# Sequence 0 turned un-normalised, its 1/rms multiplied in at the read-outs of the in-projection

## Chip, core and metric

The kernel runs on one core of a Trainium2 chip. The metric is the device time of one execution in microseconds (us), lower is better. Before the change the median of three runs is 1139.7 us.

## What is computed

One layer of a bidirectional encoder, applied with the same weights to two sequences of 512 tokens and 1024 channels (x_prompt is sequence 0, x_sample sequence 1), all in f32:

```
def rms_norm(x, g):
    y = xf * lax.rsqrt(jnp.mean(xf * xf, axis=-1, keepdims=True) + EPS)
    return (y * g).astype(x.dtype)

h = rms_norm(x, norm_attn_g)
proj = h @ w_in                  # 1024 -> 2304 columns: qa ka va qb kb vb
ya = global_gqa_attention(rope(rms_norm(qa)), rope(rms_norm(ka)), va)
yb = neighbourhood_attention(qb, kb, vb, nat_rel_bias, rows)
y = jnp.concatenate([rms_norm(ya, out_norm_a_g), rms_norm(yb, out_norm_b_g)], axis=-1)
x = x + y @ w_out
u = jnp.square(jax.nn.relu(rms_norm(x, norm_mlp_g) @ w_up))
return rms_norm(x + u @ w_down, final_norm_g)
```

## The kernel before

Tokens lie on partitions in eight tiles of 128, four for each sequence (NT = 8, TPB = 4). A product of two f32 matrices is made of three matmuls of rounded parts (hi times hi, lo times hi, hi times lo, in a one-pass type), the lines L1066, L1067 and L1068. So both factors have to be split into a hi and a lo part. ScalarE makes the hi parts, VectorE the lo parts.

**The input norm and the first products.** For a tile t of sequence 0 the steps are: SP issues the DMAs of its two halves of 512 columns into `pj` (L682); ScalarE squares the tile with a running sum (L905) and takes the root of the mean (L909); VectorE makes the reciprocal (L936) and multiplies the tile by it into `xn` (L945); TensorE turns `xn` in eight blocks of 128x128 against the identity `ident`, four to a PSUM bank (L966, function `pe_norm`); ScalarE casts each bank to the hi part of `hT` (L928), VectorE subtracts for the lo part (L951). Gains are multiplied into the weights: a weight piece is 128 rows (channels) of `w_in` by 512 columns; ScalarE makes `w_hi` (L1007), VectorE `w_lo` (L1016). `norm_alone` writes out this order for tiles 0 to 3 on ScalarE and VectorE, with the split of weight piece t behind tile t. Here and below, turn t means the eight transposes of tile t.

TensorE's first wave is written out by hand: turn 0; then for i = 0 to 3: turn i + 1 (up to 3), and the products that tile i and weight piece i make possible, namely 1, 3, 5 and 7 products of three matmuls (product groups 0 to 3, with 3, 9, 15 and 21 matmuls). The three products of group 1 are, in order: tile 1 with piece 0, tile 1 with piece 1, tile 0 with piece 1. Group 2 begins with tile 2 and pieces 0, 1, 2. Then turn 4, and `run_block` goes through the remaining pieces.

**Blocks.** `BLOCKS` lists the stages of the in-projection. Block 0: qa of sequence 0, banks 0 to 3. Block 1: qa of sequence 1, banks 4 to 7. Block 2: ka and va of both (256 columns). Block 3: qb, block 4: kb, with channels on partitions and tokens along the row, four banks for sequence 0 (0 to 3) and four for sequence 1 (4 to 7), in the order 0, 4, 1, 5, ... Blocks 5 and 6: vb. Each block has eight weight pieces (k = 0 to 7). Sequence 1's tiles are normed and turned between the pieces of block 0 (`woven`). At a block's last piece ScalarE and VectorE read the banks out (`take`): in qb and kb ScalarE takes sequence 0 and VectorE sequence 1, elsewhere even and odd banks. `after_tm` and `after_fm` are TensorE's waits for those read-outs when the next block reuses a bank. POOL's `stage` rounds qb and kb of a head pair later.

**DMA.** All transfers are issued by SP, in one queue. The four raw slots of weight pieces (`w_raw`) are freed by the VectorE split; `load_piece` waits for that from the fifth piece on, and everything behind it in SP's program waits too. The order at the start: both halves of tile 0, w_gain, ident, then tile 1, piece 0, tile 2, piece 1, tile 3, pieces 2 and 3, tiles 4 to 7, pieces 4 to 7.

## Time and profile before

| | us |
|---|---|
| median of 3 runs | 1139.7 (1139.53 to 1140.13) |
| profiled execution, its own time | 1139.17 |
| its span, first to last instruction | 1137.4 |
| TensorE busy | 1119.9 (98%) |
| VectorE busy | 767.7 (67%) |
| ScalarE busy | 535.6 (47%) |
| POOL busy | 186.1 (16%) |

The profile is of one execution. Times in its views count from the first instruction. Busy time of TensorE is modelled at the ends of matmuls: in a stream each is shown longer than the distance to the next, so distances between starts are the better measure. A plain f32 matmul is recorded as two, a transpose and a matmul of rounded parts as one. DMA issues are rows of SPq, and their duration is that of the issue; the time to landing is in a view of its own.

### The profile page before, as it was taken

Reading aid. Unit: us, or ns where it says so; the run is one execution under the profiler, and the core shown is the slowest. Engines: PE = TensorE matmul, PEld = TensorE weight load, DVE = VectorE, ACT = ScalarE, POOL = GpSimd, SP = SyncE. Lnnn points to the kernel's source line nnn. Section 1 sums busy time; section 2 is a strip of 40 time slices with the busy share of each in tenths; the row PEclk is TensorE's granted clock in tenths of the full one; section 3 lists DMA queues with packets and bytes.
Section 4 is the critical chain, followed back from the end, with each engine's and each line's share of the span. In section 5 each row is a group of like instructions: output and inputs, shape, how many; then the busy total and the mean of one; then the engine's idle time right before and its main releaser. Section 6 shows DMA issues by size and latency. Waiting matters only on the chain.

```text
span 1137.4 us, 15392 instructions
## 1 busy us (share of the span) xinstructions
PE 1119.9 (98%) x5536; PEld 929.7 (82%) x5536; DVE 767.7 (67%) x1348; ACT 535.6 (47%) x1018; POOL 186.1 (16%) x199
## 2 busy tenths in 40 slices
PE   6999999999999999999999999999999999999997
PEld 5898888789999988888888788888888888888885
DVE  5525314477666556464977998948859769579497
ACT  6421213366676645255334446245254353452556
POOL 2430496121214000200100100001001001000012
PEclk9999999999999999999999999999999999999999
DMA  9422113475445352421210210221111112102204
GB/s 262 119 74 56 47 47 84 112 166 112 85 95 118 111 143 88 162 84 56 75 37 1 75 49 26 75 75 38 51 62 57 54 39 75 56 19 75 75 19 148
DMA packets 55387, 90.97 MB, mean 80 GB/s; under 512 B 6032, under 2 KB 23440, under 8 KB 55312
## 3 DMA queue, kind: packets, MB, share of 16 engines
q1 hardware_dynamic: 55312, 89.99, 28.5%
q8 instruction: 44, 0.72, 0.3%
q14 instruction: 31, 0.25, 0.1%
HBM read 68.97 MB, written 4.19 MB: 64 GB/s over the span
## 4 chain that ended last, share of the span: by engine, by line
PE 97%; DVE 1%; ACT 1%; issue 0%; DMA 0%; DVEq 0%; SPq 0%; ACTq 0%
PE ps L1066 27%; PE ps L1068 27%; PE ps L1067 27%; PE ps L1274 5%; PE ps L1296 2%; PE ps L966 1%; PE ps L1232 1%; PE ps L1247 1%; PE ps L1233 1%; PE ps L1216 1%; PE ps L1259 1%; DMA pj<-x_prompt 0%; PE ps L1193 0%; PE ps L1451 0%; PE ps L1311 0%
## 5 line engine op out<-in xcount | busy, mean ns | idle before, releaser
L1066 PE MATMUL ps<-w_hi,uv_hi 128*128 128x512 f32 x448 | 178.6, 399 | 0.2 <-issue 0.2
L1066 PE MATMUL ps<-hT,w_hi 128*128 128x512 f32 x448 | 177.1, 395 | 0.0
L1068 PE MATMUL ps<-w_hi,uv_lo 128*128 128x512 f32 x448 | 176.8, 395 | 0.0
L1068 PE MATMUL ps<-hT,w_lo 128*128 128x512 f32 x448 | 176.8, 395 | 0.0
L1067 PE MATMUL ps<-hT,w_hi 128*128 128x512 f32 x448 | 176.8, 395 | 0.0
L1067 PE MATMUL ps<-w_lo,uv_hi 128*128 128x512 f32 x448 | 176.7, 394 | 0.0
L1016 DVE SCALAR_TENSOR_TENSOR w_lo<-w_raw,w_gain,w_hi 128x512 fp32r<-128x512 f32 (+1 forms) x88 | 69.8, 798 | 140.6 <-ACT w_hi L1007 139.8
L2051 DVE TENSOR_TENSOR xr<-ps,xr 128x512 f32<-128x512 f32 x220 | 138.0, 683 | 7.4 <-PE ps L1068 7.0
L1007 ACT ACTIVATE w_hi<-w_raw,w_gain 128x512 fp32r<-128x512 f32 (+1 forms) x88 | 61.4, 704 | 171.5 <-PE ps L1068 168.0
L1066 PE MATMUL ps<-w_hi,hT 128*128 128x512 f32 (+1 forms) x320 | 120.4, 376 | 0.3 <-DVE hT L951 0.2
L1068 PE MATMUL ps<-w_hi,hT 128*128 128x512 f32 (+1 forms) x320 | 119.1, 372 | 0.0
L1067 PE MATMUL ps<-w_lo,hT 128*128 128x512 f32 (+1 forms) x320 | 119.0, 372 | 0.0
L2533 POOL TENSOR_TENSOR sqf<-sqf 128x512 f32<-128x512 f32 x16 | 20.4, 1297 | 502.9 <-DVE w_lo L1896 502.9
L1066 PEld LDWEIGHTS ps<-w_hi,uv_hi 128*128 128x128 f32 x448 | 84.3, 188 | 22.1 <-issue 2.3
L1067 PEld LDWEIGHTS ps<-w_lo,uv_hi 128*128 128x128 f32 x448 | 84.4, 188 | 20.4 <-issue 1.0
L1068 PEld LDWEIGHTS ps<-w_hi,uv_lo 128*128 128x128 f32 x448 | 84.3, 188 | 19.8
L1068 PEld LDWEIGHTS ps<-hT,w_lo 128*128 128x128 f32 x448 | 84.3, 188 | 19.8
L1067 PEld LDWEIGHTS ps<-hT,w_hi 128*128 128x128 f32 x448 | 84.3, 188 | 19.8
L1066 PEld LDWEIGHTS ps<-hT,w_hi 128*128 128x128 f32 x448 | 84.3, 188 | 19.6
L1917 DVE TENSOR_TENSOR uv_lo<-sqf,uv_hi 128x512 fp32r<-128x512 f32 x112 | 75.1, 713 | 14.7 <-ACT uv_hi L1589 13.9
L1589 ACT CAST uv_hi<-sqf 128x512 fp32r<-128x512 f32 x112 | 64.6, 616 | 22.1 <-DVE sqf L2039 20.1
L1497 ACT CAST w_hi<-turn 128x512 fp32r<-128x512 f32 x64 | 36.6, 617 | 75.3 <-PE ps L1068 75.3
(164 smaller groups left out, 2005.9 us busy)
## 6 DMA issues: line engine op xcount, KB each, us to landing
w_raw<-w_in SPq DMA_DIRECT2D x48, 256.0 KB, 2.7
stk<-stg SPq DMA_DIRECT2D x32, 256.0 KB, 3.6
w_raw<-w_out SPq DMA_DIRECT2D x32, 256.0 KB, 2.6
raw<-w_down SPq DMA_DIRECT2D x32, 256.0 KB, 2.9
turn<-w_down SPq DMA_DIRECT2D x32, 256.0 KB, 2.8
w_raw<-w_up SPq DMA_DIRECT2D x24, 256.0 KB, 2.7
turn<-w_up SPq DMA_DIRECT2D x24, 256.0 KB, 2.9
raw<-w_up SPq DMA_DIRECT2D x24, 256.0 KB, 3.0
```

What stands on the lines that cost most here:

```text
L1007: ins = nc.scalar.mul(w_hi[:, slot, 0:width], src, g)
L1016: ins = nc.vector.scalar_tensor_tensor(w_lo[:, slot, 0:width], src, g, hi, ALU.mult, ALU.subtract)
L1066: nc.tensor.matmul(out, a_hi, b_hi, start=first, stop=False, skip_group_check=onto)
L1067: nc.tensor.matmul(out, a_hi, b_lo, start=False, stop=False, skip_group_check=onto)
L1068: return nc.tensor.matmul(out, a_lo, b_hi, start=False, stop=last, skip_group_check=onto)
L1274: mm = nc.tensor.matmul(ps[a_out_bank(u // TPB)][:, q * VW:(q + 1) * VW], turn_slot(u - q + k)[:, q * P:(q + 1) * P], pj[:, b * TPB + k, c ...
L1296: mm = nc.tensor.matmul(ps[OB_BANK][:, q * VW:(q + 1) * VW], turnB[:, n % PTB_SLOTS, k * P:(k + 1) * P], v, start=(k == 0), stop=(k == nk ...
L1497: nc.scalar.copy(w_hi[:, n % W_SLOTS, :], weight(c, False, v, kt)).then_inc(hi_split, 1)
L1589: nc.scalar.copy(uv_hi[:, u_slot(c, name), kt, :], u_source(name, kt)).then_inc(uv_hi_ready, 1)
L1917: nc.vector.tensor_tensor(uv_lo[:, u_slot(c, name), kt, :], u_source(name, kt), uv_hi[:, u_slot(c, name), kt, :].bitcast(F32), ALU.subtrac ...
L2051: nc.vector.tensor_tensor(dst, ps[v % 2 * 4 + t][:, :], dst, ALU.add).then_inc(c_added, 1)
L2533: nc.gpsimd.tensor_tensor(sqf[:, 1, kt, :], sqf[:, 1, kt, :], sqf[:, 0, kt, :], ALU.subtract).then_inc(s4_done, 1)
```

## The change

Sequence 0's tiles are turned as they land, straight from `pj`, and split into hi and lo without having been divided by their RMS. The reciprocals are multiplied in when the banks of the in-projection are read out.

- In `pe_norm`, turn t of sequence 0 waits for the left half of the tile (`x_left`) ahead of its first four transposes and for the right half (`x_right`) ahead of the last four. It waits for no VectorE result. Sequence 1 is normed as before.
- ScalarE's squares of tiles 0 to 3 (`act_square_raw`) come one tile behind the casts and the weight split, and one root (`act_root_raw`) serves four tiles. VectorE makes the four reciprocals in one instruction and, in one more, a diagonal matrix of them for each tile (`diag`).
- `turn_rstd`: at block 1, k = 3, TensorE multiplies a matrix of ones (set by POOL) by the four diagonals, which puts 1/rms of token j in column j of each row of bank 0. VectorE copies it to `rstd_row` one piece later. These four products are plain f32 ones.
- Read-outs with tokens on partitions (qa, ka, va, vb of sequence 0) multiply by the tile's reciprocals in place of a copy. For qb and kb VectorE now reads out sequence 0, times `rstd_row`, and ScalarE sequence 1; the waits of TensorE and of POOL's `stage` follow. TensorE's first product of block 2 in bank 0 waits for the copy of the row.
- SP's order: left half of tile 0, ident, right half, w_gain, piece 0, and from then on a tile and a piece in turn. For tiles 4 to 7 the piece comes first.

```diff
@@ SP
-            load_x_halves(0)
+            load_x_half(0, 0)
+            sp.dma_start(ident[:, :], ident_c).then_inc(const_landed, 16)
+            load_x_half(0, 1)
             sp.dma_start(w_gain[:, :, :].rearrange("p m d -> p (m d)"), w_gains).then_inc(gain_landed, 16)
-            sp.dma_start(ident[:, :], ident_c).then_inc(const_landed, 16)
-            for t in range(1, TPB):
-                load_x_halves(t)
-                load_pieces(t - 1, t)
-            load_pieces(TPB - 1, RAW_SLOTS)
-            for t in range(TPB, NT):
-                load_x_halves(t)
-            load_pieces(RAW_SLOTS, NT)
+            load_pieces(0, 1)
+            for t in range(1, NT):
+                if t >= TPB:
+                    load_pieces(t, t + 1)
+                load_x_half(t, 0)
+                load_x_half(t, 1)
+                if t < TPB:
+                    load_pieces(t, t + 1)
@@ pe_norm
-            pe.wait_ge(xn_ready, norm_no(m, t) + 1)
+            raw = m == 0 and t < TPB
+            if not raw:
+                pe.wait_ge(xn_ready, norm_no(m, t) - TPB + 1)
...
             for j in range(2):
+                if raw:
+                    pe.wait_ge((x_left, x_right)[j][t], 16)
                 for d in range(4):
+                    cols = slice((4 * j + d) * P, (4 * j + d + 1) * P)
                     last = nc.tensor.transpose(norm_bank(m, t, j)[:, d * P:(d + 1) * P],
-                                               xn[:, t % 2, (4 * j + d) * P:(4 * j + d + 1) * P], ident[:, :])
+                                               pj[:, t, cols] if raw else xn[:, t % 2, cols], ident[:, :])
@@ TensorE
+            def turn_rstd(k):
+                if k == ROW_TURN:
+                    pe.wait_ge(all_ones, 1)
+                    pe.wait_ge(diag_ready, 1)
+                    pe.wait_ge(act_evac, 1)
+                    for t in range(TPB):
+                        last = nc.tensor.matmul(ps[0][:, t * P:(t + 1) * P], ones[:, :], diag[:, t, :], start=True,
+                                                stop=True)
+                    last.then_inc(row_turned, 1)
+            def after_row(pos, bank):
+                if bank == 0:
+                    pe.wait_ge(row_copied, 1)
+                after_tm(0)(pos, bank)
             run_block(0, after_norm0)
-            run_block(1, after_norm0)
-            run_block(2, after_tm(0))
+            run_block(1, after_norm0, turn_rstd)
+            run_block(2, after_row)
@@ ScalarE
+        def act_square_raw(act, t):
+            norm_src_wait(act, 0, t)
+            nc.scalar.activation(qkb_0[:, 2 * t:2 * t + 2, :].rearrange("p h c -> p (h c)"), pj[:, t, 0:D], ACT.Square,
+                                 accum_out=stat[:, 0, t, 0:1]).then_inc(sumsq, 1)
...
-            norm_alone(0, 0, square, hT_hi_of, lambda n: act_split(act, n, n % W_SLOTS, width_of(n), piece_gain(n)))
+            for t in range(TPB):
+                hT_hi_of(0, t)
+                act_split(act, t, t % W_SLOTS, width_of(t), piece_gain(t))
+                if t:
+                    act_square_raw(act, t - 1)
+            act_square_raw(act, TPB - 1)
+            act_root_raw(act)
@@ VectorE, take
                     if blk.what in ("qb", "kb"):
-                        ins = nc.vector.tensor_scalar(qkb[1][:, part, :], ps[bank][:, :],
-                                                      QSCALE if blk.what == "qb" else 1.0, None, ALU.mult)
+                        dve.wait_ge(row_copied, 1)
+                        ins = nc.vector.scalar_tensor_tensor(qkb[0][:, part, :], ps[bank][:, :],
+                                                             QSCALE if blk.what == "qb" else 1.0, rstd_row[:, :],
+                                                             ALU.mult, ALU.mult)
+                    elif bank < TPB:
+                        dve.wait_ge(rstd_ready, TPB)
+                        ins = nc.vector.tensor_scalar(evac_dst(blk, bank), src, rstd[:, 0, bank, 0:1], None, ALU.mult)
@@ VectorE
+                        if i == 1 and k == ROW_TURN + 1:
+                            dve.wait_ge(row_turned, 1)
+                            nc.vector.tensor_copy(rstd_row[:, :], ps[0][:, :]).then_inc(row_copied, 1)
...
-            norm_alone(0, 0, norm, hT_lo_of, lambda n: dve_split(dve, n, n % W_SLOTS, width_of(n), piece_gain(n)))
+            for t in range(TPB):
+                hT_lo_of(0, t)
+                dve_split(dve, t, t % W_SLOTS, width_of(t), piece_gain(t))
+            dve.wait_ge(rms_ready, TPB)
+            nc.vector.reciprocal(rstd[:, 0, 0:TPB, 0], rms[:, 0, 0:TPB, 0]).then_inc(rstd_ready, TPB)
+            dve.wait_ge(rstd_ready, TPB)
+            dve.wait_ge(const_landed, 16)
+            nc.vector.tensor_tensor(diag[:, :, :], over(ident[:, :], 1, TPB), over(rstd[:, 0, 0:TPB, 0], 2, P),
+                                    ALU.mult).then_inc(diag_ready, 1)
```

What SP issues first. Before, both halves of tile 0, the gains, ident; here x_prompt is sequence 0, x_sample sequence 1, and w_in a weight piece:

```order
L682 DMA pj<-x_prompt 128x1x512 x2
L701 DMA w_gain<-w_gains 128x16
L702 DMA ident<-ident_c 128x128
L682 DMA pj<-x_prompt 128x1x512 x2
L693 DMA w_raw<-w_in 128x512
L682 DMA pj<-x_prompt 128x1x512 x2
L693 DMA w_raw<-w_in 128x512
```

and with the change:

```order
L690 DMA pj<-x_prompt 128x1x512
L709 DMA ident<-ident_c 128x128
L690 DMA pj<-x_prompt 128x1x512
L711 DMA w_gain<-w_gains 128x16
L701 DMA w_raw<-w_in 128x512
L690 DMA pj<-x_prompt 128x1x512 x2
L701 DMA w_raw<-w_in 128x512
L690 DMA pj<-x_prompt 128x1x512 x2
```

ident has moved between the halves of tile 0, and piece 0 ahead of tile 1.

ScalarE at its start, before: the squares (L905) stand ahead of the casts (L928) that make `hT`:

```order
L905 ACTIVATE xn,stat<-pj 128x1024
L909 ACTIVATE rms<-stat,eps 128x1
L905 ACTIVATE xn,stat<-pj 128x1024
L909 ACTIVATE rms<-stat,eps 128x1
L928 CAST hT<-ps 128x4x128 x2
L1007 ACTIVATE w_hi<-w_raw,w_gain 128x512
```

and with the change, where L926 is the square and L932 the root of all four tiles:

```order
L951 CAST hT<-ps 128x4x128 x2
L1025 ACTIVATE w_hi<-w_raw,w_gain 128x512
L951 CAST hT<-ps 128x4x128 x2
L1025 ACTIVATE w_hi<-w_raw,w_gain 128x512
L926 ACTIVATE qkb,stat<-pj 128x1024
L951 CAST hT<-ps 128x4x128 x2
L1025 ACTIVATE w_hi<-w_raw,w_gain 128x512
L926 ACTIVATE qkb,stat<-pj 128x1024
L951 CAST hT<-ps 128x4x128 x2
L1025 ACTIVATE w_hi<-w_raw,w_gain 128x512
L926 ACTIVATE qkb,stat<-pj 128x1024 x2
L932 ACTIVATE rms<-stat,eps 128x4
```

Each square now stands behind the cast and the weight split of the tile after it.

TensorE in block 1, with the change, between pieces 3 and 4; the lines of the three matmuls are now L1084 to L1086:

```order
L1084 MATMUL ps<-w_hi,hT 128x512
L1085 MATMUL ps<-w_lo,hT 128x512
L1086 MATMUL ps<-w_hi,hT 128x512
L1190 MATMUL ps<-diag,ones 128x128 x4
L1084 MATMUL ps<-w_hi,hT 128x512
```

The four row products are new there; before, the matmuls of piece 4 followed those of piece 3.

## Rows read from the trace of the kernel before

**Rows 1.** The page: TensorE's busy time, and its busy tenths in 40 slices.
```profile
PE 1119.9 (98%) x5536; PEld 929.7 (82%) x5536; DVE 767.7 (67%) x1348; ACT 535.6 (47%) x1018; POOL 186.1 (16%) x199
...
PE   6999999999999999999999999999999999999997
```

**Rows 2.** Waits of TensorE: who for whom, us in total, times, longest.
```profile
PE ps L966 <- DVE xn L945: 9.0, 3, 8.3
PE ps L1247 <- DVE negmax L2315: 1.1, 2, 0.8
```

**Rows 3.** Chain that ended last, 0 to 20 us: start, us, what.
```profile
1.47 4.16 DMA pj<-x_prompt
...
5.65 1.16 ACT xn L905 x2
...
7.36 0.76 DVE xn L945
```

**Rows 4.** Timeline of TensorE: start, us, operation, idle before and releaser.
```profile
8.26 1.94 PE L966 MATMUL ps<-ident,xn 128*128 128x128 f32 x8 [8.26 <-DVE xn L945]
10.59 1.85 PE L966 MATMUL ps<-ident,xn 128*128 128x128 f32 x8 [0.39 <-DVE xn L945]
...
13.85 1.10 PE L966 MATMUL ps<-ident,xn 128*128 128x128 f32 x8 [0.36 <-DVE xn L945]
15.13 0.47 PE L1066 MATMUL ps<-w_hi,hT 128*128 128x512 f32 x1 [0.19 <-DVE hT L951]
...
17.31 1.03 PE L966 MATMUL ps<-ident,xn 128*128 128x128 f32 x8
18.10 0.48 PE L1066 MATMUL ps<-w_hi,hT 128*128 128x512 f32 x1
```

**Rows 5.** Stretch: PE, PEld, DVE, ACT, POOL busy; PEclk, DMA share, GB/s.
```profile
8.26:12.54 4.28, 3.79 (x16) 3.14 (x17) 2.77 (x5) 4.01 (x9) 0.00 (x0) 1.00 1.07 262
```

**Rows 6.** Timeline of SP: start and us of DMA issues.
```profile
0.73 1.31 SPq L682 DMA_DIRECT2D pj<-x_prompt  x2
...
6.27 0.59 SPq L693 DMA_DIRECT2D w_raw<-w_in  x1
...
8.12 1.06 SPq L693 DMA_DIRECT2D w_raw<-w_in  x2
```

**Rows 7.** Issue to landing, us (last number), of issues at 0.73, 2.71, 6.27, 8.12.
```profile
pj<-x_prompt SPq DMA_DIRECT2D x1, 256.0 KB, 3.6
ident<-ident_c SPq DMA_DIRECT2D x1, 64.0 KB, 3.4
w_raw<-w_in SPq DMA_DIRECT2D x1, 256.0 KB, 5.4
w_raw<-w_in SPq DMA_DIRECT2D x1, 256.0 KB, 6.2
```

**Rows 8.** Timeline of ScalarE and VectorE, 8 to 15 us.
```profile
10.24 0.59 ACT L928 CAST hT<-ps 128x512 fp32r<-128x512 f32 x1 [0.21 <-PE ps L966]
...
10.72 0.73 ACT L1007 ACTIVATE w_hi<-w_raw,w_gain 128x512 fp32r<-128x512 f32 x1
...
11.65 0.74 DVE L1016 SCALAR_TENSOR_TENSOR w_lo<-w_raw,w_gain,w_hi 128x512 fp32r<-128x512 f32 x1
...
12.71 1.05 ACT L928 CAST hT<-ps 128x512 fp32r<-128x512 f32 x2
```

**Rows 9.** Timeline of TensorE in the tail; L1451 is a plain f32 product.
```profile
1123.63 0.40 PE L1068 MATMUL ps<-w_hi,uv_lo 128*128 128x512 f32 x1
1123.86 1.02 PE L1451 MATMUL ps<-xr,ident 128*128 128x512 f32 x2
...
1124.95 0.39 PE L1067 MATMUL ps<-w_lo,uv_hi 128*128 128x512 f32 x1
```

**Rows 10.** Groups of VectorE by line: count, busy us, mean ns, idle before.
```profile
L1016 DVE SCALAR_TENSOR_TENSOR w_lo<-w_raw,w_gain,w_hi 128x512 fp32r<-128x512 f32 (+1 forms) x88 | 69.8, 798 | 140.6 <-ACT w_hi L1007 139.8
...
L1880 DVE TENSOR_SCALAR qkb<-ps 128x512 f32<-128x512 f32 x8 | 5.5, 682 | 3.3 <-PE ps L1068 3.2
```

58 lines of the change are left out of this document (34 added, 24 removed).

## Prediction

> **What bounds the kernel now.** I read the page first. TensorE is busy for 98% of the span, in all but the first and the last of the forty slices [rows 1]. So a microsecond is to be had in two ways only: TensorE gets less work, or it starts its unbroken run earlier. The list of waits says where it does not run: of its idle time 9.0 us lie before the turns of the normalised tiles, 8.3 of them in one piece, at the start [rows 2]. The chain of waits over the first 20 us names what fills that piece: tile 0 lands at 5.63 (1.47 + 4.16), ScalarE squares it (1.16), the root and the reciprocal follow, VectorE scales it (0.76), and the turn starts at 8.26 [rows 3, 4]. The timeline of TensorE then shows four more turns and the first products [rows 4]: 10.59 turn 1, 13.85 turn 2, 15.13 the nine matmuls of group 1 (2.18 us until turn 3), 17.31 turn 3, 18.10 group 2 (fifteen matmuls). From 15.13 on TensorE has no gap that the list of waits would show, so **the start of group 2, 18.10, is my yardstick**: whatever moves it moves everything behind it, since the only later wait of TensorE over 1 us in that list, 1.1 on VectorE in the attention part [rows 2], is for an engine that itself follows TensorE. From 8.26 to 12.54 the DMA engines are full (share 1.07, 262 GB/s) [rows 5], which will matter.
>
> A second reading of the same rows: eight turns take 1.94 and 1.85 us at first, 1.10 at 13.85 [rows 4], though the granted clock is printed as full [rows 5]. That is the ratio of TensorE's two levels, 1.2 and 2.4 GHz. It was low for the 3.9 us from its first work until about 12.2, and high after.
>
> **What goes away.** Four squares, roots, reciprocals and scalings no longer stand ahead of the turns of sequence 0. The squares and one root come back behind ScalarE's casts, where nobody on the path waits: their results are wanted at the first read-out, far behind. The four scalings of VectorE (0.76 each) vanish. What is late next is the data itself.
>
> **When the data lands.** Tile 0's left half was issued at 0.73 and landed 3.6 later, at 4.3; ident needed 3.4 from issue to landing [rows 6, 7]. It is now second in SP's queue. As it is 64 KB behind 256 it lands about 4.6 (bounds: 4.3, were it free, and 1.47 + 3.4 = 4.9), so turn 0 starts at 4.7. The right half follows ident and lands near 5.9. For the tiles behind I count bytes, since the engines are full and the queue is worked off in order. Weight piece 1 landed at 6.27 + 5.4 = 11.7, piece 2 at 8.12 + 6.2 = 14.3 [rows 6, 7]. What stood ahead of and in piece 1 (three tiles, ident, gains, two pieces) is what now stands ahead of and in the right half of tile 2, so that half lands at 11.7. In the same way the right half of tile 3 lands at 14.3, and tile 1's one such step (2.6 us) before tile 2's, at 9.1. Each x tile after the first is thus later than before by one weight piece.
>
> **TensorE's new start.** Turn 0 ends near 7.0; turn 1's right half runs from 9.1 to 10.1 at the low level (half of 1.85). The weight chain behind it: cast 0.59, w_hi 0.73, w_lo 0.74 [rows 8], so piece 1 is split at 12.1 or 12.2. Product group 0 fits between 10.1 and 11.4 even at the low level. Turn 2's right half, from 11.8, takes half of 1.10: 12.3. So group 1 starts at 12.3 rather than 15.13, bound by a landing and with the weight split just ahead of it. Then 2.18 for it and 0.79 for turn 3 (17.31 to 18.10) [rows 4]: 15.3. Tile 3 has landed by 14.3. Piece 2's chain on ScalarE (square 1.2, two casts 1.05, w_hi 0.73, then w_lo 0.74 [rows 3, 8]) ends at 15.1, and only the third product of group 2 wants it. **18.10 - 15.3 = 2.8 us** earlier. If transfers come 0.3 sooner, the weight split binds and it is 3.0. I take off 0.1 for executions in which the level is still low at 11.8 (turn 2's second half would cost 0.5 more).
>
> **What SP now does in another order.** It waits for a free raw slot ahead of each of pieces 4 to 7, with x tiles of sequence 1 queued behind each such wait. The waits end when pieces 0 to 3 are split (about 9, 12, 15, 18), while the DMA engines still have work queued until about 18, so they don't run dry; the bytes until piece 7 are the same. Turn 4 wants its tile landed, squared, scaled by 23.7; the tile lands at about 18 and its chain takes 2.5. Nothing is charged. Without that cover it would be up to 1 us.
>
> **What is added on the path.** Four products of 128 x 128 stand in TensorE's stream in block 1, in plain f32. The nearest row is the plain f32 product of the tail: from the matmul at 1123.63 to the one at 1124.95 there are 1.32 us, in which stand that matmul (0.23), one plain product of 512 columns, recorded as two halves of 0.43, and one more matmul (0.23) [rows 9]. So 0.86 us for 512 columns, and the four products have 512 columns together: **0.87 us**. The bounds are 0.44 (as cheap as the turns, 0.11 for 128 columns) and 1.3 (each of the eight halves bound by its 0.19 us weight load with no overlap). I take 0.87, the same type and kind.
>
> The Trainium skill (TensorE: Matmul & The Clock Gate, Terms) says that the transpose mode is 4 times faster for FP32 than an ordinary product. Here the turn takes 0.11 us for 128 columns and the plain product 0.22, so this trace shows 2 times. By the page the four products would cost 1.74, and the time would be 0.9 later than I forecast.
>
> **What is added beside the path.** The diagonal (one 128x512 operation of VectorE, some 0.8) and its reciprocal lie after piece 3's split, and TensorE wants them 25 us later. The copy of the row (0.69) lies in block 1 and is wanted a few us later, at bank 0 of block 2. The read-outs of block 0, 2 and vb do the same pass with a scale. For qb and kb the two engines swap sequences and VectorE multiplies by the row: an operation with two inputs took it 798 ns on average, a read-out with a constant 682 [rows 10]. Four of them, one in 1.4 us, are hidden by the products of the next bank. Zero, all of it; the POOL waits follow the swap. If VectorE were the bound there it would be eight times 0.12, 1 us.
>
> **Sum.** -2.8 + 0.1 + 0.9 = -1.8 us. On the profiled execution (span 1137.4, its own time 1139.17) that gives 1137.4. The median of the runs shown, 1139.7, is 0.5 above that execution, and the result will be a median too: **1139.7 - 1.8 = 1137.9 us**. A measurement of this kernel can tell about 0.2% (2.3 us) from no change, so the forecast itself lies within it.
>
> **Rivals.**
> - *More gain than I count.* Landings 0.3 sooner, the row products at 0.6: -3.0 + 0.6 = -2.4, 1137.3. For it: ident and the gains are small. Against: the byte count is of this very queue. Chance 0.17.
> - *The level rises late.* In the change TensorE pauses from 7.0 to about 7.8, and again for landings before turn 2, where it paused for 0.4 before. If the rise comes at the end of group 1, turn 2's half costs 0.5 more and the nine matmuls twice 2.18 less what is saved, about 2.0 more: 2.5 in all, hence -2.8 + 2.5 + 0.9 = +0.6, 1140.3; if it comes halfway, 1138.9. I take 1139.0 for this case. Chance 0.12.
> - *Plain f32 product at four times the turn.* 1138.8. Only the page speaks for it. Chance 0.05.
> - *Slower.* The same mechanism, further: the pauses keep the level low through turn 3 and group 2. Group 2 (15 matmuls of 0.235) would take 3.5 more and turn 3 0.8 more, on top of the 2.5: -2.8 + 6.8 + 0.9 = +4.9, 1144.6. It decides from the place where the rise falls: later than the middle of group 2 the kernel is slower by over 0.2%. Against it: the level rose before across a pause of 0.4 and another soon after didn't drop it. Chance 0.04.
> - *It doesn't start earlier.* Something I take as covered holds the first wave (the weight split of piece 1, SP's waits), and the gain only pays for the row products: 1139.7. Chance 0.07.
>
> The Trainium skill (TensorE: Matmul & The Clock Gate, What's actually happening) says that the low level is the default, that activity releases it, and that the watch runs free of the kernel's start. By it the moment of the rise differs from run to run, and the second and fourth cases may show in single executions; the trace of one execution can't show that.
>
> **The numbers.** Forecast 1137.9 has 0.55. Faster by over 0.2% (below 1137.4): the first rival and a small part of the forecast's own spread, 0.21. Slower by over 0.2%: 0.05. The rest, 0.74, is within. The range 1137.1 to 1139.1 holds the forecast, the first rival, the f32 case and half of the late rise.
>
> **What the profile after would show.** The first turn at 4.7 and in halves; turn 2's right half starting on a landing near 11.7; group 1 at 12.3, group 2 at 15.3; from there a constant lead of 2.8 until block 1, then 1.9 after four products that take 0.87; no wait of TensorE at bank 0 of block 2. If group 2 starts at 15.3 and the total is not 1.8 shorter, something later took it back, which I hold impossible. The prediction is wrong if the turns of tile 2 still take 0.2 each, or if group 1 starts on a weight split later than 12.3.

## The result, and the profile of the changed kernel

| | median us (lowest to highest) | executions |
|---|---|---|
| before | 1139.79 (1139.53 to 1140.13) | 6 |
| changed | 1144.37 (1141.12 to 1145.15) | 6 |

The ratio is 1.0034, with a 95% interval of 1.0021 to 1.0047. The changed kernel is slower by 0.34%, some 4 us (4.6 between the medians); 1137.9 was forecast. A second measurement gave it 1141.27 (1139.25 to 1145.71, 12 executions) against 1139.62, ratio 1.0018 (1.0008 to 1.0028). It is slower in both, and its executions spread over 4 to 6.5 us where those of before spread over 0.6 to 2. That spread is part of the finding.

The profiled execution is the lowest of the first six: its own time is 1141.12, its span 1139.1, against 1137.4 before. The page, TensorE's busy time and its tenths in 40 slices, to be read beside [rows 1]:

```profile
PE 1122.6 (99%) x5544; PEld 930.6 (82%) x5544; DVE 765.3 (67%) x1343; ACT 535.3 (47%) x1015; POOL 185.9 (16%) x200
...
PE   7999999999999999999999999999999999999997
```

TensorE has eight matmuls more, as four plain f32 products are recorded in halves, and its first slice went from 6 to 7 tenths: it does begin earlier. Its waits (who for whom, us in total, times, longest), to be read beside [rows 2]:

```profile
PE ps L994 <- DMA ident<-ident_c: 4.5, 1, 4.5
PE ps L994 <- DMA pj<-x_prompt: 2.2, 4, 1.5
PE ps L994 <- DVE xn L968: 1.3, 1, 1.3
```

Of the 9.0 us before turns, 6.7 are left at the start, and now they are waits for DMAs. The third row is new. L968 scales the tiles of sequence 1, whose norm the change leaves as it was, and before there was no wait for such a tile. The timeline of TensorE, to be read beside [rows 4]:

```profile
4.49 1.12 PE L994 MATMUL ps<-ident,pj 128*128 128x128 f32 x4 [4.49 <-DMA ident<-ident_c]
...
8.41 1.12 PE L994 MATMUL ps<-ident,pj 128*128 128x128 f32 x4 [1.48 <-DMA pj<-x_prompt]
...
12.82 0.66 PE L994 MATMUL ps<-ident,pj 128*128 128x128 f32 x4 [0.28 <-DMA pj<-x_prompt]
13.24 0.48 PE L1084 MATMUL ps<-w_hi,hT 128*128 128x512 f32 x1
...
16.20 0.48 PE L1084 MATMUL ps<-w_hi,hT 128*128 128x512 f32 x1
...
37.15 1.09 PE L994 MATMUL ps<-ident,xn 128*128 128x128 f32 x8 [1.34 <-DVE xn L968]
...
52.21 1.05 PE L1190 MATMUL ps<-diag,ones 128*128 128x128 f32 x8
53.02 0.48 PE L1084 MATMUL ps<-w_hi,hT 128*128 128x512 f32 x1
```

Turn 0 starts at 4.49 and group 2 at 16.20, 1.9 us before the 18.10 of before. Late in block 0 stands the surprise: turn 7 comes after 1.34 us in which TensorE has nothing to do. I laid the matmuls of the two traces side by side, each against its counterpart. The changed kernel leads by 1.90 us from group 2 on and by 0.34 behind turn 7. The first product of block 1 costs it 0.17 more, and the row products 0.82, so that it is 0.65 late behind them. By 210 us it is 1.1 late, and 1.4 at the last product, with no wait that is new. Of the 0.43 between the row and 210 us some 0.3 turned out to be systematic (the row, below).

The chain of waits names what holds turn 7 (start, us, what):

```profile
22.56 0.67 DVE w_lo L1034
23.25 9.78 DMA w_raw<-w_in
33.10 0.58 issue
33.68 1.06 ACT hT L951 x2
34.74 1.06 ACT xn L916 x2
35.82 0.30 ACT rms L920
36.34 0.77 DVE xn L968
37.15 1.09 PE ps L994 x8
```

To be read backwards: turn 7 waits for tile 7 scaled by VectorE, that for ScalarE's root and square, these for the two casts of turn 5, and the casts for a weight piece. A tile of x has nothing to do with a weight piece. The timeline of ScalarE shows why (start, us, operation, idle before and releaser):

```profile
28.85 0.29 ACT L920 ACTIVATE rms<-stat,eps 128x1 f32<-128x1 f32 x1
33.05 0.72 ACT L1025 ACTIVATE w_hi<-w_raw,w_gain 128x512 fp32r<-128x512 f32 x1 [3.91 <-DMA w_raw<-w_in]
33.68 1.06 ACT L951 CAST hT<-ps 128x512 fp32r<-128x512 f32 x2
34.63 1.07 ACT L916 ACTIVATE xn<-pj 128x1024 f32<-128x1024 f32 x1
```

ScalarE works in order. It stands 3.91 us before the split of **weight piece 8**, whose own products begin only with block 1, at 40.96, and behind it are queued the casts of turn 5 and the square of tile 7. The square is what TensorE will want next. The same place in the kernel before, ScalarE's timeline and the issue of piece 8 (at 25.80, last number: us to landing):

```profile
30.23 0.30 ACT L909 ACTIVATE rms<-stat,eps 128x1 f32<-128x1 f32 x1
30.66 0.72 ACT L1007 ACTIVATE w_hi<-w_raw,w_gain 128x512 fp32r<-128x512 f32 x1
```

```profile
w_raw<-w_in SPq DMA_DIRECT2D x1, 256.0 KB, 4.8
```

Before, ScalarE was free at 30.53 and the piece landed at 30.64, a tenth later: ScalarE had no slack, and a wait too short to show in the view. With the change ScalarE is there at 29.14 and the piece lands at 33.0. It is issued 2.55 us earlier (23.25) and lands 2.4 later, as the queue takes 9.8 us to get to its end rather than 4.8.

TensorE did have slack there before. VectorE's scaling of tile 7 and TensorE's turn 7:

```profile
33.95 0.75 DVE L945 TENSOR_SCALAR xn<-pj,rstd 128x1024 f32<-128x1024 f32 x1
```

```profile
37.55 1.04 PE L966 MATMUL ps<-ident,xn 128*128 128x128 f32 x8
```

Tile 7 was ready at 34.70, 2.85 us ahead of its turn. A lead of 1.90 uses up two thirds of that and leaves 0.95. Tile 7 is now ready at 37.11, 2.41 later, so TensorE has to come out some 1.5 later against its counterpart. That is what the side-by-side reading shows (1.90 less 0.39 at the first transpose of turn 7); the idle time in the view, 1.34, is shorter because ends of matmuls are modelled. So it takes both, the earlier start and the later landing. With the lead of 2.8 that was forecast, nothing would have been left even at the old landing.

### The profile page after: what moved, and what is told of

It is laid out like the page before. It is cut to its first block, busy times and chain, and to the rows that moved or that the text cites. A ratio compares the mean times of both kernels' runs of the same rounds, so it can differ in the third digit from the quotient of the medians.

```text
span 1139.1 us, 15426 instructions
## 1 busy us (share of the span) xinstructions
PE 1122.6 (99%) x5544; PEld 930.6 (82%) x5544; DVE 765.3 (67%) x1343; ACT 535.3 (47%) x1015; POOL 185.9 (16%) x200
## 3 DMA queue, kind: packets, MB, share of 16 engines
q1 hardware_dynamic: 55312, 89.99, 28.5%
## 4 chain that ended last, share of the span: by engine, by line
PE 95%; DMA 1%; ACT 1%; DVE 1%; issue 0%; SPq 0%; DVEq 0%; ACTq 0%
PE ps L1084 27%; PE ps L1085 27%; PE ps L1086 27%; PE ps L1309 5%; PE ps L1331 2%; PE ps L1267 1%; PE ps L1282 1%; PE ps L1268 1%; PE ps L1251 1%; PE ps L1294 1%; PE ps L994 1%; DMA w_raw<-w_in 1%; DMA pj<-x_prompt 1%; PE ps L1228 0%; PE ps L1486 0%
## 5 line engine op out<-in xcount | busy, mean ns | idle before, releaser
L1084 PE MATMUL ps<-w_hi,uv_hi 128*128 128x512 f32 x448 | 178.5, 399 | 0.2 <-issue 0.2
L1084 PE MATMUL ps<-hT,w_hi 128*128 128x512 f32 x448 | 177.1, 395 | 0.0
L1086 PE MATMUL ps<-hT,w_lo 128*128 128x512 f32 x448 | 176.8, 395 | 0.0
L1086 PE MATMUL ps<-w_hi,uv_lo 128*128 128x512 f32 x448 | 176.8, 395 | 0.0
L1084 PE MATMUL ps<-w_hi,hT 128*128 128x512 f32 (+1 forms) x320 | 121.0, 378 | 0.0
L1086 PE MATMUL ps<-w_hi,hT 128*128 128x512 f32 (+1 forms) x320 | 119.2, 372 | 0.0
L1084 PEld LDWEIGHTS ps<-w_hi,uv_hi 128*128 128x128 f32 x448 | 84.3, 188 | 22.1 <-issue 2.0
L1086 PEld LDWEIGHTS ps<-w_hi,uv_lo 128*128 128x128 f32 x448 | 84.3, 188 | 19.9
L1086 PEld LDWEIGHTS ps<-hT,w_lo 128*128 128x128 f32 x448 | 84.3, 188 | 19.9
L1084 PEld LDWEIGHTS ps<-hT,w_hi 128*128 128x128 f32 x448 | 84.3, 188 | 19.8
```

Of the source, the lines that this page charges most:

```text
L1084: nc.tensor.matmul(out, a_hi, b_hi, start=first, stop=False, skip_group_check=onto)
L1086: return nc.tensor.matmul(out, a_lo, b_hi, start=False, stop=last, skip_group_check=onto)
```

## The experiments

Three theories stood at the start. **A, data late**: the transfers of pieces and tiles late in block 0 come later and are wanted earlier; whatever brings piece 8 sooner, or takes its split out of ScalarE's way, removes the wait before turn 7. **B, the row**: the row products and what hangs on them in blocks 1 and 2 cost more than their 0.82 us. **C, the level**: TensorE's low level lasts longer in executions with many short waits at the start.

The table is for looking up; the sections say what follows. Piece 3, tile 7 and piece 8 are landings, "wait" is TensorE's before turn 7, all in us in the profiled execution. The median and the ratio to before (95% interval) are those of all executions. Chips differ between the groups of runs, so medians of different groups are best compared by their ratios.

| kernel | piece 3 | tile 7 | piece 8 | group 2 | wait | median | ratio |
|---|---|---|---|---|---|---|---|
| before | 15.2 | 23.7 | 30.6 | 18.10 | 0 | 1139.79 | |
| before_again | 15.5 | 24.0 | 31.1 | 18.07 | 0 | 1140.06 | 1.0005 (0.9995 to 1.0015) |
| changed | 16.3 | 28.3 | 33.0 | 16.20 | 1.3 | 1144.37 | 1.0034 (1.0021 to 1.0047) |
| same_again | 17.0 | 32.0 | 36.2 | 16.76 | 3.9 | 1141.27 | 1.0018 (1.0008 to 1.0028) |
| tables_late | 16.2 | 26.8 | 27.9 | 17.21 | 0 | 1139.59 | 1.0000 (0.9992 to 1.0009) |
| old_order | 15.4 | 24.0 | 31.1 | 16.62 | 0 | 1140.74 | 1.0009 (1.0001 to 1.0018) |
| no_row | 15.7 | 27.8 | 33.0 | 15.76 | 1.7 | 1139.36 | 0.9996 (0.9988 to 1.0005) |
| defer_split | 16.4 | 29.8 | 33.7 | 16.07 | 0 | 1140.40 | 1.0006 (0.9997 to 1.0016) |
| late_turned_row | 16.9 | 28.7 | 29.9 | 16.64 | 0 | 1139.11 | 0.9993 (0.9983 to 1.0002) |
| late_busy | 16.6 | 29.6 | 30.0 | 16.13 | 0 | 1139.32 | 0.9996 (0.9987 to 1.0005) |
| late_old_order | 17.7 | 26.4 | 31.0 | 18.15 | 0 | 1140.60 | 1.0006 (0.9997 to 1.0016) |
| late_all | 16.2 | 27.7 | 28.1 | 16.14 | 0 | 1139.38 | 1.0000 (0.9991 to 1.0009) |
| row_twice | 15.9 | 27.2 | 29.0 | 15.85 | 0 | 1139.42 | 0.9997 (0.9987 to 1.0006) |
| before_late | 15.7 | 23.8 | 28.5 | 17.98 | 0 | 1139.51 | 0.9998 (0.9989 to 1.0007) |

### The changed kernel once more

No edit.

> The changed kernel once more, for a second trace and for the spread of its executions. Theory A (data late): in the first trace group 2 started 1.9 us earlier, but piece 8 of the weights landed at 33.0, ScalarE waited 3.9 us for it with the work for turn 7 queued behind, and TensorE lost 1.35 us before turn 7; the executions differ because the DMA rate of the first 35 us differs. Then the landing of tile 7's last half (28.3) and of piece 8 (33.0) should move by a microsecond or more in this trace, the wait before turn 7 with them, and the total with the wait; the executions spread over 3 us or more around 1144. Theory C (TensorE's level): the landings are the same and the extra time is in turns or matmuls at half speed.

Its profiled execution is its highest, 1145.71, and so shows what a high one is made of. TensorE's timeline around turn 7, and three stretches (PE, PEld, DVE, ACT, POOL busy; PEclk; DMA share; GB/s):

```profile
40.28 1.97 PE L994 MATMUL ps<-ident,xn 128*128 128x128 f32 x8 [3.94 <-DVE xn L968]
41.89 0.78 PE L1084 MATMUL ps<-w_hi,hT 128*128 128x512 f32 x1
42.47 0.63 PE L1085 MATMUL ps<-w_lo,hT 128*128 128x512 f32 x1
42.89 0.63 PE L1086 MATMUL ps<-w_hi,hT 128*128 128x512 f32 x1
```

```profile
36.30:40.28 3.98, 0.04 (x2) 0.01 (x1) 2.93 (x6) 3.95 (x9) 0.00 (x0) 0.99 0.51 133
40.28:43.60 3.32, 3.32 (x12) 3.03 (x13) 3.32 (x6) 2.35 (x6) 0.00 (x0) 0.50 0.52 122
43.60:46.00 2.40, 2.40 (x11) 1.94 (x11) 1.34 (x3) 1.53 (x3) 0.00 (x0) 1.00 0.76 175
```

The wait is 3.94 instead of 1.34, as piece 8 landed at 36.2. And it brings a second loss: after the pause the granted clock is 0.50, the lower of the two levels, for 3.3 us. The turn takes 1.97 instead of 1.09 and the products behind it stand 0.58 and 0.42 apart, where 0.31 and 0.23 are usual. The sum: 1.34 ahead at group 2, 3.94 waited, 1.7 lost at the low level and 0.80 at the row products make 5.1 late at 57.5 (side by side with before: 5.1 as well), and 6.3 at the last product. So A has its mechanism; C has a part in it, but as a consequence of A's wait and not at the start. Of the 18 executions of the changed kernel four were recorded with a mean granted clock of 0.996 or 0.997 over the whole span, all of them at 1144.49 or above; no execution of the kernel before lies below 0.998. That fits such a low stretch in them too. But 1144.55 and 1144.21 have 0.998, so it is not the whole of the high times.

### The tables' transfers behind those of block 1's pieces

`tables_late`: the changed kernel, in which the transfers of rope, the q/k gains, the mask and the bias tables are issued behind weight pieces 8 to 15. Nothing else is moved.

```
+            load_pieces(NT, NT + BH)
             sp.dma_start(rope[...], rope_c).then_inc(pool_landed, 16)
             ...
             for h in range(BH):
                 sp.dma_start(bias_raw[:, h, :], src).then_inc(pool_landed, 16)
-                load_pieces(NT + h, NT + h + 1)
```

> The changed kernel, but SP issues rope, the q/k gains, the mask and the eight bias tables after weight pieces 8 to 15 and not among them (1.8 MB less ahead of pieces 8 to 15; POOL needs the tables far later). Theory A: piece 8 lands near 30.5 and TensorE's wait before turn 7 is gone, so 1139.8 at most in the best executions and a median 1.4 to 4 us below the changed kernel's, with a small spread. Theory B (the added work on the path, row products and read-outs, makes the kernel slow) and theory C: no difference from the changed kernel, 1144.

ScalarE's split of piece 8:

```profile
29.63 0.72 ACT L1025 ACTIVATE w_hi<-w_raw,w_gain 128x512 fp32r<-128x512 f32 x1 [0.61 <-PE ps L1086]
```

Piece 8 lands at 27.9 (near 30.5 was expected), ScalarE waits 0.61 for TensorE and no longer for a DMA, and TensorE's wait before turn 7 is gone. The median is 1139.59 against 1141.27 for the changed kernel on the same chip, and equal to before. That is what A says. The edit also takes 0.9 MB of tables out from ahead of piece 8, and tile 7 lands 1.5 earlier in this trace, so that by itself it doesn't tell which of the two TensorE was held by; `defer_split` does. B has the row products still in it and would have left the time where it was: as the main cause it falls.

It doesn't get below before, because the start gives less than forecast. Here the level rose only at 14.9, so group 2 came at 17.21, 0.9 ahead, and the row products took that back.

### The same in the kernel before

`before_late`: the same edit in the kernel before. `before_again`: the kernel before, no edit.

> Control: the kernel before, with SP's tables behind pieces 8 to 15. In its trace piece 8 landed at 30.6, 3 us ahead of the need, and TensorE never waited for it. So theory A expects no change: 1139.7 within 0.3. A gain here would mean that the late tables are worth something of their own, and that tables_late did not cure a wait that the change brought.

> The kernel before once more, for a second trace. The changed kernels' matmuls lagged 0.1 to 0.9 us more behind the first trace of it by the end than at 60 us, without a wait. If that is in the executions and not in the change, this trace too differs from the first by some tenths over the same stretch. Transfers: the four x tiles and four pieces that landed by 15.2 in the first trace land anywhere from 15 to 18 here, as in the changed kernels, and the span still moves by less than 1 us, because the first products stand behind the norm.

Piece 8 lands at 28.5 instead of 30.6 and the time is unchanged (0.9998, 0.9989 to 1.0007). In the kernel before these transfers cost nothing; they cost only once TensorE is 2 us earlier. `before_again` is a look at the noise: from group 2 to 640 us both keep their distance to the trace of before within 0.06 us, and from there `before_again` falls 0.35 behind and `before_late` gains 0.25, with no wait that differs. A few tenths in the later half can't be given a cause by comparing two traces; a step in the first 210 us can.

It also showed a late level in the kernel before (TensorE's timeline):

```profile
12.57 0.76 PE L1066 MATMUL ps<-w_hi,hT 128*128 128x512 f32 x1
...
13.99 1.08 PE L966 MATMUL ps<-ident,xn 128*128 128x128 f32 x8
15.10 0.47 PE L1066 MATMUL ps<-w_hi,hT 128*128 128x512 f32 x1
```

Product group 0 at the low level takes 0.57 and 0.42 between starts, and yet group 1 stands at 15.10 as in [rows 4] (15.13): before, VectorE's and ScalarE's chain set the start, and it covered the slow matmuls. The changed kernel has no such cover.

### The order of x and weights of before

`old_order`: the changed kernel, with x tiles and weight pieces issued in the order of before.

```
-            load_pieces(0, 1)
-            for t in range(1, NT):
-                if t >= TPB:
-                    load_pieces(t, t + 1)
+            for t in range(1, TPB):
                 load_x_half(t, 0)
                 load_x_half(t, 1)
-                if t < TPB:
-                    load_pieces(t, t + 1)
+                load_pieces(t - 1, t)
+            load_pieces(TPB - 1, RAW_SLOTS)
+            ...
```

> The changed kernel with the old order of x tiles and weight pieces in SP's program (tile 1, piece 0, tile 2, piece 1, tile 3, pieces 2 and 3, tiles 4 to 7, pieces 4 to 7; ident still between the halves of tile 0). Theory A: the same bytes stand ahead of piece 8, so it lands late too, and the median stays within 1 us of the changed kernel's 1144. If the interleaving itself slows the queue (the x tiles took 1.2 to 1.4 us a half and not 1.1), tile 7 and piece 8 land 1 to 2 us sooner here and the time falls to 1141 or 1142. Theories B and C: 1144.

TensorE's timeline:

```profile
10.67 0.77 PE L1085 MATMUL ps<-w_hi,hT 128*128 128x512 f32 x1 [1.20 <-DVE w_lo L1035]
...
13.65 0.49 PE L1085 MATMUL ps<-w_hi,hT 128*128 128x512 f32 x1
```

Tile 7 lands at 24.0 and piece 8 at 31.1, as in the kernel before, and the wait before turn 7 is gone. Theory A as I had put it, by the bytes ahead of piece 8, missed here; the other branch, that the interleaving itself is slower, came true. At the start TensorE now waits 1.2 for the split of piece 0 instead of for x, and group 2 stands at 16.62, 0.4 later. So the interleaved order buys 0.4 us at the start and costs the transfers behind it 2 to 4. Its median, 1140.74, is 0.5 below the changed kernel's and 1.1 above before. Side by side with before it leads by 1.5 at group 2 and loses 0.3 at the first product behind turn 4, which needs weight piece 4 (landed at 24.6, as before): the earlier start meets that transfer too. It leads by 0.35 behind the row products, and is 0.6 late at the end; the profiled execution, 1139.96, is also one of its lower ones. What the higher ones wait for wasn't traced.

### The row left out

`no_row`: the four products of ones and diagonals are left out, and VectorE copies the diagonals themselves in place of the row. So q and k of the neighbourhood attention in sequence 0 are multiplied by the diagonals, mostly zeros, in place of 1/rms; all other work is done.

```
-            run_block(1, after_norm0, turn_rstd)
+            run_block(1, after_norm0)
```

> The changed kernel without the four row products of TensorE: VectorE copies the diagonals themselves into rstd_row, so qb and kb of sequence 0 are multiplied by a wrong row and the output is not the reference's. It measures the price of the products: 0.87 us by the forecast, 0.82 by the first trace (the lag of the matmuls behind those of the kernel before grows by that in block 1). The total falls by 0.8 to 0.9, within the spread of the executions. Theory B has them cost 2 us or more, with what waits for the row.

The wait stays:

```profile
PE ps L994 <- DVE xn L968: 1.7, 1, 1.7
```

So B isn't what holds turn 7. But it has more in it than I forecast. The step of 0.82 at 52 us is gone, and with it most of the 0.43 that the changed kernel loses between there and 210 us: here it is 0.15. The place of it is in block 2, whose matmuls have 256 columns. TensorE's timeline at two matmuls of it, with 140 starts from one to the other; before, then the changed kernel:

```profile
69.22 0.28 PE L1066 MATMUL ps<-w_hi,hT 128*128 128x256 f32 x1
...
85.83 0.28 PE L1068 MATMUL ps<-w_hi,hT 128*128 128x256 f32 x1
```

```profile
70.01 0.28 PE L1084 MATMUL ps<-w_hi,hT 128*128 128x256 f32 x1
...
86.81 0.28 PE L1086 MATMUL ps<-w_hi,hT 128*128 128x256 f32 x1
```

16.61 us against 16.80, or 118.7 ns from one start to the next against 120.0. In `no_row` it is 118.7 again. All other traces of the changed kind show 120.0, and all three of the kernel before 118.7. Over the 192 matmuls of block 2 that is 0.25 us. The first product behind the row adds 0.07. So the row costs about 1.15 us, not 0.82. Why a block that begins 11 us behind the row runs 1% slower isn't known: `late_turned_row` and `row_twice` below narrow it a little. The median falls by 1.9 against the changed kernel on this chip, where 0.8 to 0.9 was expected; with executions between 1137.1 and 1141.7 I put no cause to the other 0.75.

### The split of piece 8 moved behind the norm of tile 7

`defer_split`: the transfers stay as changed. In ScalarE's and VectorE's programs the split of piece 8 is moved to the place of piece 9's.

```
-                            act_split(act, n, n % W_SLOTS, width_of(n), piece_gain(n))
+                            for late in () if n == 8 else (8, 9) if n == 9 else (n,):
+                                act_split(act, late, late % W_SLOTS, width_of(late), piece_gain(late))
```

> The changed kernel with one thing moved: ScalarE and VectorE make the hi and lo parts of weight piece 8 one step later, after the casts of turn 5, the square and the scaling of tile 7 (k = 5 of block 0), together with piece 9. SP's queue is as in the changed kernel, so piece 8 still lands as late, at 33 or later. Theory A says that this landing costs time only because the cast of turn 6 and the square of tile 7 stand behind the split of piece 8 in ScalarE's order: then TensorE's wait before turn 7 (1.3 and 3.9 us in the two traces) is gone, the median falls to 1139.7, and the spread is under 2.5 us. If TensorE is held by the late bytes themselves (tile 7 or piece 8 wanted at once), the wait stays, and so does the median of 1141 to 1144.

ScalarE, and then TensorE at the first product of block 1:

```profile
33.76 0.72 ACT L1025 ACTIVATE w_hi<-w_raw,w_gain 128x512 fp32r<-128x512 f32 x1 [1.78 <-DMA w_raw<-w_in]
```

```profile
39.67 0.47 PE L1084 MATMUL ps<-w_hi,hT 128*128 128x512 f32 x1 [0.36 <-DVE hT L974]
```

This is the run that separates the late transfer from the order in which ScalarE meets it. Piece 8 lands at 33.7, later than in the changed kernel's first trace, and still TensorE doesn't wait before turn 7, for the square and root of tile 7 (30.50 to 31.98) are done by then. A small wait comes in its place, as the queue of work behind the two splits is now late for block 1. The median is 1140.40 and the ratio 1.0006 (0.9997 to 1.0016), against 1.0018 for the changed kernel: most of the loss is back, as far as runs on two chips can be compared. The median of 1139.7 and the spread under 2.5 us that were expected did not come: the executions lie between 1139.2 and 1142.7.

### The row by transposes

`late_turned_row`: `tables_late`, and the row of 1/rms is made by transposing four matrices, each of which holds in all 128 columns of a row the 1/rms of that row's token, instead of by plain f32 products.

```
-                        last = nc.tensor.matmul(ps[0][:, t * P:(t + 1) * P], ones[:, :], diag[:, t, :], start=True,
-                                                stop=True)
+                        last = nc.tensor.transpose(ps[0][:, t * P:(t + 1) * P], diag[:, t, :], ident[:, :])
...
-            nc.vector.tensor_tensor(diag[:, :, :], over(ident[:, :], 1, TPB), over(rstd[:, 0, 0:TPB, 0], 2, P),
-                                    ALU.mult).then_inc(diag_ready, 1)
+            nc.vector.tensor_copy(diag[:, :, :], over(rstd[:, 0, 0:TPB, 0], 2, P)).then_inc(diag_ready, 1)
```

> tables_late (the tables of SP behind pieces 8 to 15), and the row of 1/rms made by turning: VectorE writes 1/rms across 128 columns in place of the diagonal, and TensorE turns these four tiles against ident in place of four plain products with ones. Forecast of the rows: a plain f32 product of 128 columns 0.22 us, a turn 0.11, so the lag that the matmuls get at this place falls from 0.82 to 0.44 and the total by 0.4 against tables_late (1139.2). If the products cost what they do for another reason (the change of operands, the weight load), the lag stays at 0.8.

```profile
50.90 0.60 PE L1190 MATMUL ps<-ident,diag 128*128 128x128 f32 x4
51.26 0.48 PE L1084 MATMUL ps<-w_hi,hT 128*128 128x512 f32 x1
```

From the transposes to the next product there are 0.36 us, where the plain products took 0.81 (52.21 to 53.02). By the measure that gave 0.82 before, the lag that the matmuls get here is 0.36, and 0.44 at the second one behind, as expected. The 0.43 behind the row stay. It is the lowest median of all, 1139.11 (1139.2 was expected), at 0.9993 (0.9983 to 1.0002) of before. That is not more than no change, but it is the form I would use.

`row_twice` is this kernel with each of the four transposes done twice, to see what block 2's pace hangs on.

```
-                    for t in range(TPB):
+                    for t in (0, 1, 2, 3, 0, 1, 2, 3):
```

> Tables' transfers behind the pieces of block 1, the row of 1/rms made by transposes, and each of the four transposes is done twice: eight instructions of TensorE in block 1, k = 3. The question is what makes the 256-column matmuls of block 2 stand 120.0 ns apart in all kernels that make the row, and 118.7 ns where it isn't made. If it follows from the number of TensorE's instructions ahead (their place in the program), eight transposes may bring 118.7 back or keep 120.0, but with one or the other the first product behind the row changes as well; if it follows from the row being made at all, block 2 stays at 120.0. The eight transposes take 0.79 us where four took 0.36, and the median is 0.4 above that of the kernel with four, 1139.5, within 0.2% of before.

```profile
50.10 1.04 PE L1190 MATMUL ps<-ident,diag 128*128 128x128 f32 x8
50.89 0.48 PE L1084 MATMUL ps<-w_hi,hT 128*128 128x512 f32 x1
```

Eight transposes take 0.79 us, the time that the four f32 products took in their eight halves, and the median is 1139.42. Block 2 keeps its 120.0 ns with four transposes, with eight, and with f32 products. So neither the form nor the number of the instructions sets the pace; what `no_row` lacks besides them are TensorE's three waits ahead of them, and these weren't taken out by themselves.

### Idle products ahead of the data

`late_busy`: `tables_late`, and TensorE multiplies ones by ones 7 times before ident lands and 4 times behind turn 0, into a bank that is overwritten.

```
+            def keep_busy(n):
+                for _ in range(n):
+                    nc.tensor.matmul(ps[0][:, 0:P], ones[:, :], ones[:, :], start=True, stop=True)
+            pe.wait_ge(all_ones, 1)
+            keep_busy(7)
             pe.wait_ge(const_landed, 16)
...
             pe_norm(pe, 0, 0)
+            keep_busy(4)
```

> tables_late with eleven idle products of TensorE (ones by ones, into bank 0 which is cleared later): seven from about 1.2 us until ident lands and four after turn 0. Theory A gives the start of group 1 to the landing of tile 2 (12.7 to 13.0) and, in tables_late, to turns and products at the low level until 12 to 14.9. With earlier work the level should be high from about 8 on: product group 0 takes 0.7 and not 1.3, turn 2's halves 0.5 each, group 1 starts within 0.6 of tile 2's landing, 13.2, and group 2 at 16.2 rather than 17.2; total 0.5 to 1 us below tables_late. If the level doesn't matter, no change.

```profile
1.14 3.36 PE L1142 MATMUL ps<-ones 128*128 128x128 f32 x14 [1.14 <-POOL ones L2482]
...
10.11 0.47 PE L1084 MATMUL ps<-w_hi,hT 128*128 128x512 f32 x1
...
12.67 0.66 PE L994 MATMUL ps<-ident,pj 128*128 128x128 f32 x4 [0.29 <-DMA pj<-x_prompt]
13.08 0.48 PE L1084 MATMUL ps<-w_hi,hT 128*128 128x512 f32 x1
```

The level is high from 6.0 on. The turns behind that and group 0 take half, and group 1 still stands at 13.08, where the changed kernel had it at 13.24: the right half of tile 2 lands in between. Against that trace C is worth 0.2 us at the start; what binds is the data. Against `tables_late`, where the level rose only at 14.9, group 2 comes 1.1 earlier (16.13, as expected, for 17.21). Of the 0.5 to 1 us expected in the median 0.3 came (1139.32 for 1139.59), and the intervals of the two overlap.

### Two combinations

`late_old_order` is `tables_late` with the order of before; `late_all` is `tables_late` with the row by transposes and the idle products.

> tables_late with the old order of x tiles and weight pieces. In four traces of the new order the transfers up to piece 3 had landed at 15.7 to 17.0, in two of the old order at 15.2 and 15.4, though the bytes are the same. If the order makes the difference, piece 3 lands at 15.2 to 15.5 here too; the first product then waits for piece 0 (9.0) and its split until about 10.6, group 1 starts at 13.6, and the total is that of tables_late within 0.5 us. If the difference was chance, piece 3 lands between 15.7 and 17.

> The three edits that helped, together, on the changed kernel: tables of SP behind pieces 8 to 15, row of 1/rms by turning, and the eleven idle products of TensorE. If they add, each from its own place (no wait on piece 8; 0.4 us of row; level high from 6 us on), the median is 1138.7: late_turned_row's 1139.1 less the 0.3 to 0.6 of the idle products. That is 0.8 to 1.1 us below the kernel before, 0.1%. If the row's gain and the early level are one and the same chance of the executions, 1139.1.

`late_old_order` missed. In the profiled execution, its highest, TensorE waited 2.1 us for splits (`w_lo`), 1.4 for that of piece 0 and 0.7 at 28.36 for that of piece 4, and group 2 came at 18.15; piece 3 landed at 17.7, though the order is that of before, which had it at 15.2. So late landings in the first 17 us can come without the new order of x and weights (ident still stands between the halves of tile 0 here). The median, 1140.60, is not within 0.5 of that of `tables_late` either. `late_all` has the lowest span, 1135.9, and a median of 1139.38, no better than before: 7 of its 11 executions are above 1139.0, three of them above 1141. 1138.7, or at worst 1139.1, was expected. Two of those three were recorded with a mean granted clock of 0.996 and 0.997, so a stretch at the low level may have come back in them; none of them was traced. None of these versions beats the kernel before by more than the measurement can tell.

## Why the prediction was wrong

**What held.** Turn 0 was forecast for 4.7 and started at 4.49, on ident, in halves. The row products were forecast at 0.87 and took 0.81 where they stand. The Trainium skill's factor of four between the transpose mode and an ordinary FP32 product (TensorE: Matmul & The Clock Gate, Terms), which would have made them 1.74, did not show: four products took 0.81, four transposes 0.36 and eight 0.79, a factor of about two. The read-outs were free: no wait of TensorE stands at block 2's first bank, and VectorE's read-out with the row as second input took no longer than the one of before with a constant, 682 [rows 10]:

```profile
L1926 DVE SCALAR_TENSOR_TENSOR qkb<-ps,rstd_row 128x512 f32<-128x512 f32 x8 | 5.3, 678 | 1.9 <-PE ps L1086 1.9
```
The diagonal took VectorE 0.69 at 20.53, with nobody waiting. Two slips in the working changed nothing: eight halves bound by weight loads of 0.19 would take 1.5 us and not 1.3, and the timeline shows three more turns behind the first, not four.

**Step "When the data lands" gave 0.9 us too much.** By counting bytes I had the right half of tile 2 at 11.7, and the chain has the end of its transfer at 12.78 (6.26 + 6.52). The count was right as a count: what was transferred by then is the same set of ten transfers as by 11.7 before. It just took 1.1 us longer. The halves of tiles 1 and 2 came 1.2 to 1.6 us after the transfer before them, where the trace of before has 1.0 to 1.1. One trace gave me one rate, and I treated it as a constant. So group 1 started at 13.24 rather than 12.3 and group 2 at 16.20 rather than 15.3: a lead of 1.9 in place of 2.8. In the other traces with the new order it is between 0.9 and 2.3.

**Step "What SP now does in another order" failed.** "Nothing is charged" rested on two statements: the DMA engines don't run dry, and the bytes until piece 7 are the same. Both are so (their share from 12 to 32 us is 1.04 before and 1.06 changed). The conclusion isn't. For one thing, an equal busy share is not an equal rate. From 12 to 28.3 us the share is 1.06 in both traces, but 300 GB/s were moved before and 271 with the change.

The twelve transfers behind piece 3 (tiles 4 to 7 and pieces 4 to 7) took 10.7 to 11.1 us from its landing to the last of theirs in all five traces with the order of before, `late_old_order` among them, and 10.6 to 14.9 in the nine with the new order. In the first trace of the changed kernel they took 11.97 where they had taken 10.92. Of the 2.4 us by which piece 8 came later, 1.1 had arisen up to piece 3, 1.05 arose here and 0.2 behind. For another, I took "the queue never runs dry" for "nobody waits", and looked at tile 4 alone. Pieces 4 to 7 now stand ahead of tile 7, which moved its landing from 23.7 to 28.3, and piece 8, behind all of them and the tables, from 30.6 to 33.0. The rows I had read stopped at piece 2. One more, ScalarE's split of piece 8 at 30.66, would have shown that ScalarE had no slack there, and two more that TensorE had 2.85 us: even a landing at the old time is late for ScalarE once the work ahead of it moves up, though not yet for TensorE. With the lead of 1.9 and the landing 2.4 later TensorE lost 1.5 at turn 7, where I had put nothing.

**Step "What is added on the path" was short by 0.3.** The products themselves held; the 0.07 behind them and the 0.25 in block 2 are in no row of before.

**The yardstick.** "Whatever moves it moves everything behind it" was the sentence that hid this, and "which I hold impossible" its echo. The engine was never waiting behind group 2 *at the old pace*. A start that comes earlier meets the transfers of block 0 at their old times or, as here, later. The lead was constant only until turn 7, not until block 1.

**The rivals.** The slower case was priced at 1144.6 and given 0.04, by the low level lasting through group 2. The median came out near it, by another mechanism: a wait late in block 0, and the drop of the level that follows a long one. At the start the level rose at 11.9 in the changed kernel's first trace and at 12.9 in the second. The number is no confirmation of the rival. That the moment of the rise differs between executions did show: in the two traces of the kernel before, whose TensorE began at 8.26 and 8.22, it was 12.2 and 14.1.

**What stays open.** Of the 4.6 us between the two medians, the trace of the lowest execution accounts for its own 1.7. For the rest I have one other trace (1145.71: wait 3.9, low level 1.7), and the inference that the others lie between, since the edits that take the wait away take most of the excess with it. But those edits were measured against a changed kernel at 1141.27, 1.7 us above before; none was measured against the 1144.37 of the first measurement. Its high executions were not traced, and why it lies 3 us above the second isn't known. Why the same bytes take 1 to 2.5 us longer in the first 17 us of most changed kernels is open as well: by `late_old_order`, one trace, the order of x and weights is not its only cause. And so is why block 2 runs slower where the row is made.

## What to carry to other kernels

When a stage is made to start earlier, go through every later wait for a transfer, not only the next one, and compare its landing with the moment at which the engine *would now* ask for it; in an in-order engine the piece it waits for may be one that nobody needs yet, with urgent work queued behind. Moving transfers past each other in a full queue decides who is late, and can change the rate, even where the engines stay equally busy and the bytes are the same. The executions of the kernel before, whose start hangs on ScalarE and VectorE, spread over 0.6 to 2.2 us; those of the versions whose start hangs on landings spread over 2 to 6.5.

## What the runs showed of the hardware

- The same transfers, issued at nearly the same times, landed over a wide range: piece 3, with the same bytes ahead of it, at 15.2 to 17.7 us in fourteen traces.
- In a full queue a transfer issued 2.55 us earlier landed 2.4 later. From issue to landing piece 8 took 4.8 us before, 9.8 changed, and 12.4 in the second trace of the changed kernel.
- Weight pieces that follow one another landed 0.6 us apart (pieces 4 to 7 of before: 24.24, 24.85, 25.48, 26.10); behind an x half they took 0.5 to 0.8 in the first traces of both kernels. x halves took 1.0 to 1.1 before, up to 2.1 in the first 17 us of changed kernels (tile 1 in `late_busy`), and once 2.6 (tile 7 in `same_again`). All of them are 256 KB.
- At the same busy share of the DMA engines, 1.06 from 12 to 28.3 us, 300 GB/s were moved before and 271 changed.
- TensorE's granted clock was at full up to a pause of 3.94 us (0.99 over it), 0.50 for the 3.3 us after it, and 1.00 again; after a pause of 1.34 it stayed at 1.00.
- A plain f32 product of 128 columns took 0.20 us, a transpose of as many 0.09 to 0.10 (four in a row: 0.81 and 0.36; eight transposes: 0.79).
- Where the row is made in block 1, the matmuls of 256 columns in block 2 stand 120.0 ns apart instead of 118.7, in ten traces out of ten.
